# Order of the steps of branch A's attention on every engine, and plain copies for the first gates of branch B

## The reference

```python
proj = h @ w_in
qa, ka, va, qb, kb, vb, ga, gb = split(proj)
# branch A, 8 heads: two softmaxes (m = 0, 1) of 64 wide queries and keys per head, values 128 wide
s = einsum('bqhmd,bkhmd->bhmqk', qa, ka) * scale + bias      # keys of later chunks of 64 masked
p = softmax(s); attn = p[:, :, 0] - lam * p[:, :, 1]
ya = rmsnorm(einsum('bhqk,bkhe->bqhe', attn, va)) * subln_g * 0.8
# branch B: 16 query heads on 2 key heads, a window of 2 chunks, a sink in the denominator
merged = sigmoid(ga) * (ya @ w_branch_a) + sigmoid(gb) * (yb @ w_branch_b)
h = layer_norm(ALPHA * h + merged @ w_out)
h = layer_norm(ALPHA * h + square(relu(h @ w_ff1)) @ w_ff2)
```

## Time and profile before

| | |
|---|---|
| median of 3 runs | 1919.4 us (1918.81 to 1921.43) |
| the profiled execution | 1920.03 us, its span 1918.2 us |
| PE busy | 1827.2 us (95%) |
| DVE, ACT, POOL busy | 906.1, 609.1, 505.1 us |

### The profile page before, as it was taken

One profiled execution on the slowest core, in us unless ns is written; L12 is line 12 of the kernel. 1 busy time (PEld: TensorE's weight loads), 2 busy tenths in 40 slices (PEclk: granted clock), 3 DMA queues, 4 the chain that ended last, 5 costly groups with the idle time before them and its releaser, 6 DMA issues.

```text
span 1918.2 us, 24570 instructions
## 1 busy us (share of the span) xinstructions
PE 1827.2 (95%) x9174; PEld 1502.4 (78%) x9174; DVE 906.1 (47%) x2051; ACT 609.1 (32%) x1337; POOL 505.1 (26%) x306
## 2 busy tenths in 40 slices
PE   3999999999999997999999999999999999999995
PEld 2777777777778886888888788788888888888884
DVE  7276666666665553102422455433333333333337
ACT  4255555555556564311221211311111111111104
POOL 5111111111123442222221110633333333333324
PEclk9999999999999998999999999999999999999998
DMA  4511111111111100134322250311111111111102
GB/s 160 202 53 32 45 35 34 45 32 46 31 39 41 32 23 23 44 99 132 99 80 85 85 190 1 106 49 55 44 44 44 44 44 44 56 64 45 44 0 88
DMA packets 143108, 117.88 MB, mean 61 GB/s; under 512 B 23284, under 2 KB 129964, under 8 KB 143020
## 3 DMA queue, kind: packets, MB, share of 16 engines
q1 hardware_dynamic: 133804, 112.51, 18.5%
q10 hardware_dynamic: 9216, 4.20, 0.8%
HBM read 99.87 MB, written 21.53 MB: 63 GB/s over the span
## 4 chain that ended last, share of the span: by engine, by line
PE 80%; DVE 8%; ACT 5%; issue 2%; SPq 2%; POOL 2%; DMA 1%; POOLq 0%; DVEq 0%; ACTq 0%
PE bank L474 24%; PE bank L476 24%; PE bank L475 24%; PE bank L510 3%; PE bank L498 2%; PE bank L542 2%; ACT mix L832 1%; DVE mix L1185 1%; ACT mix L870 1%; DVE res L1121 1%; DVE mix L1236 1%; POOL w_lo L983 1%; PE bank L543 1%; SPq L336 1%; DVE o_buf L1163 1%
## 5 line engine op out<-in xcount | busy, mean ns | idle before, releaser
L474 PE MATMUL bank<-hT_hi,w_hi 128*128 128x512 f32 x1312 | 526.0, 401 | 13.8 <-POOL w_lo L983 6.4
L476 PE MATMUL bank<-hT_hi,w_lo 128*128 128x512 f32 x1312 | 513.9, 392 | 0.0
L475 PE MATMUL bank<-hT_lo,w_hi 128*128 128x512 f32 x1312 | 513.8, 392 | 0.0
L983 POOL TENSOR_TENSOR w_lo<-w_raw,w_hi 128x1024 fp32r<-128x1024 f32 x67 | 161.5, 2411 | 698.2 <-ACT w_hi L731 698.2
L474 PEld LDWEIGHTS bank<-hT_hi,w_hi 128*128 128x128 f32 x1312 | 248.1, 189 | 72.8 <-issue 9.5
L476 PEld LDWEIGHTS bank<-hT_hi,w_lo 128*128 128x128 f32 x1312 | 248.0, 189 | 53.6
L475 PEld LDWEIGHTS bank<-hT_lo,w_hi 128*128 128x128 f32 x1312 | 248.5, 189 | 48.3
L474 PE MATMUL bank<-y_hi 128*128 128x512 f32 (+1 forms) x604 | 228.0, 377 | 2.7 <-DVE small L1376 2.7
L475 PE MATMUL bank<-y_lo,y_hi 128*128 128x512 f32 (+1 forms) x604 | 225.1, 373 | 0.0
L476 PE MATMUL bank<-y_hi,y_lo 128*128 128x512 f32 (+1 forms) x604 | 225.0, 373 | 0.0
L1359 DVE TENSOR_TENSOR res<-res,bank 128x512 f32<-128x512 f32 x224 | 154.0, 687 | 141.3 <-PE bank L476 141.3
(11 more groups left out here) (133 smaller groups left out, 2636.6 us busy)
## 6 DMA issues: line engine op xcount, KB each, us to landing
w_raw<-in_w_in_dram SPq DMA_DIRECT2D x100, 256.0 KB, 3.3
w_raw<-in_w_ff_dram SPq DMA_DIRECT2D x64, 256.0 KB, 3.0
mix<-in_w_ff_dram SPq DMA_DIRECT2D x16, 1024.0 KB, 7.1
bias_rows<-bias_line SPq DMA_DIRECT2D x3, 1536.0 KB
res<-in_x_dram SPq DMA_DIRECT2D x8, 512.0 KB, 8.1
h_spill<-res SPq DMA_DIRECT2D x8, 512.0 KB, 6.8
o_spill<-o_buf ACTq DMA_DIRECT2D x64, 64.0 KB, 1.6
w_raw<-in_w_branch_b_dram SPq DMA_DIRECT2D x16, 256.0 KB, 3.9
```

Of the source, the lines that this page charges most:

```text
L474: pe.matmul(bank, lhs[0], rhs[0], start=start, stop=False)
L475: pe.matmul(bank, lhs[0], rhs[1], start=False, stop=False)
L476: return pe.matmul(bank, lhs[1], rhs[0], start=False, stop=stop)
L983: pool.tensor_tensor(w[1][:, n % 2], w_raw[:, :, :], w[0][:, n % 2].bitcast(F32), ALU.subtract).then_inc(w_lo_done, 1)
```

## The change

It has two parts.

In branch A a block's first half group now comes straight behind `block_a(0)`; then `block_a(1)` where there is one, then the transposes of the block before, then the product of the block *two* back, then a second half group where there is one. For this the transposed probabilities have a second buffer, `p_more`, in the memory of `res` rows 0 and 1, so ACT's wait for the spill of `res` now stands ahead of branch A, and `inv` has four slots instead of two. The `va` transposes move from the end of block 0 to block 1. On DVE the combination of a block moves behind the first reads of the next block's scores (`combine`). On ACT the exponentials go ahead of the copies for `i < 4`, behind them for `i >= 4`, and `out_rows` speaks of the block two back. The two products left over are made in branch B's steps 0 and 1.

In branch B the gate tiles 0 and 1 are copied out of PSUM without a sigmoid (`gate_raw`), the two halves of `gb 0` in steps 30 and 31; the sigmoid of both comes later, in place in `res`, behind the first `y_hi` copy that follows (`gates_set`). `yb_high(0)` and `yb_low(0)` are one step earlier, `yb_low(1)` stands ahead of the last low parts, the weights of `gb 2` are split right behind `yb_high(1)`, and the root moves behind the last `gb` tile.

```diff
@@ PE, branch A
                     block_a(0)
-                    prev = (h, i - 1) if i else (h - 1, NT - 1)
-                    if prev[0] >= 0:
-                        pe.wait_ge(probs_ready, prev[0] * NT + prev[1] + 1)
-                        for b in range(1 + prev[1] // 4):
-                            transposes(("pa",) + prev + (b,))
-                    if i >= 4:
-                        block_a(1)
-                    for _ in range(HALVES[i]):
+                    step = h * NT + i
+                    for piece in range(HALVES[i]):
                         group(*ORDER[6 * (h + 1) + at // 2], range(at % 2 * 4, at % 2 * 4 + 4))
                         at += 1
-                    if prev[0] >= 0:
-                        attend_a(*prev)
-                    if i == 0:
-                        pe.wait_ge(freed_act, freed(True, LAST[TILE[("va", h)]]))
-                        for b in range(2):
-                            transposes(("va", h, b))
+                        if piece == 0:
+                            if i >= 4:
+                                block_a(1)
+                            if step >= 1:
+                                pe.wait_ge(probs_ready, step)
+                                for b in range(1 + (step - 1) % NT // 4):
+                                    transposes(("pa", (step - 1) // NT, (step - 1) % NT, b))
+                            if step >= 2:
+                                attend_a((step - 2) // NT, (step - 2) % NT)
+                            if i == 1:
+                                pe.wait_ge(freed_act, freed(True, LAST[TILE[("va", h)]]))
+                                for b in range(2):
+                                    transposes(("va", h, b))
@@ DVE, branch A
+            def combine(n):
+
+                i, slot = n % NT, n % 2
+                dve.wait_ge(exp_done, n + 1)
+                if n >= 4:
+                    dve.wait_ge(sq_done, n - 3)
+                link(dve.reciprocal(inv[:, n % 4, :], sums[:, slot, :]))
+                link(dve.scalar_tensor_tensor(coef[:, slot:slot + 1], sums[:, slot, 0:1], neg_lam, inv[:, n % 4, 1:2], ALU.mult, ALU.mult))
+                p = [s_a[:, slot, m, 0:(i + 1) * P] for m in range(2)]
+                dve.scalar_tensor_tensor(p[0], p[1], coef[:, slot:slot + 1], p[0], ALU.mult, ALU.add).then_inc(probs_ready, 1)
+                dve.sem_inc(inv_ready, 1)
...
+                        if c == 0 and chunks == 2:
+                            combine(step - 1)
...
+                    if chunks == 1 and step >= 1:
+                        combine(step - 1)
@@ ACT, end of branch B
-                if s == B_STEPS - 1:
+                if s >= B_STEPS - 2:
                     act.wait_ge(yb_lo, 1)
-                    group_hi(TILE[("gb", 0)], 0)
+                    gate_raw(TILE[("gb", 0)], s - (B_STEPS - 2))
...
-                if s == B_STEPS - 3:
+                if s == B_STEPS - 4:
                     yb_high(0, B_STEPS - 5)
-            group_hi(TILE[("gb", 0)], 1)
             yb_high(1, B_STEPS - 1)
+            split_weights(TILE[("gb", 2)])
...
+            def gate_raw(n, half):
+                act.wait_ge(gemm_done, POS[(n, half)] + 1)
+                act.activation(res[:, TILES[n][1], half * HALF:(half + 1) * HALF], GEMM[POS[(n, half)] % 2][:, :], ACT.Copy).then_inc(freed_act, 1)
...
+                        if c == 2:
+                            act.wait_ge(freed_act, freed(True, POS[(TILE[("gb", 1)], 1)]))
+                            for n in range(2):
+                                act.activation(res[:, n, :], res[:, n, :], ACT.Sigmoid).then_inc(gates_set, 1)
@@ DVE, end of branch B
-                if s == B_STEPS - 2:
+                if s == B_STEPS - 3:
                     yb_low(0)
+            yb_low(1)
             probs_lo(B_STEPS - 1)
```

More of the change, by code:

```diff
@@ L312, in batch_views @@
                 c = min(4, i + 1 - 4 * b)
-                return [(pT[part][:, 4 * b:4 * b + c, :], bank[:, 0:c, :])]
+                return [(pT[i % 2][part][:, 4 * b:4 * b + c, :], bank[:, 0:c, :])]
             if kind == "pb":
@@ L818, in out_rows, with exp_a @@
                     store_rows(n - 1)
-            def prev_a(h, i, steps=NT):
-                return (h, i - 1) if i else (h - 1, steps - 1)
+            def exp_a(h, i):
+                act.wait_ge(max_ready, h * NT + i + 1)
+                for m in range(2):
+                    e = act.activation(s_a[:, i % 2, m, 0:(i + 1) * P], s_a[:, i % 2, m, 0:(i + 1) * P], ACT.Exp,
+                                       bias=neg_max[:, i % 2, m:m + 1], accum_out=sums[:, i % 2, m:m + 1])
+                e.then_inc(exp_done, 1)
+            act.wait_ge(spilled, 16 * NT)
             for h in range(A_HEADS):
@@ L825, in _ @@
                 for i in range(NT):
-                    prev = prev_a(h, i)
-                    if prev[0] >= 0:
-                        for b in range(1 + prev[1] // 4):
-                            batch_hi(("pa",) + prev + (b,))
-                    act.wait_ge(max_ready, h * NT + i + 1)
-                    for m in range(2):
-                        e = act.activation(s_a[:, i % 2, m, 0:(i + 1) * P], s_a[:, i % 2, m, 0:(i + 1) * P], ACT.Exp,
-                                           bias=neg_max[:, i % 2, m:m + 1], accum_out=sums[:, i % 2, m:m + 1])
-                    e.then_inc(exp_done, 1)
-                    for _ in range(HALVES[i]):
+                    step = h * NT + i
+                    if i < 4:
+                        exp_a(h, i)
+                    for piece in range(HALVES[i]):
                         if at % 2:
@@ L838, in _ @@
                         at += 1
[L839 to L843 removed]
+                        if piece == 0:
+                            if step >= 1:
+                                for b in range(1 + (step - 1) % NT // 4):
+                                    batch_hi(("pa", (step - 1) // NT, (step - 1) % NT, b))
+                            if i >= 4:
+                                exp_a(h, i)
+                            if step >= 2:
+                                out_rows(step - 2, (step - 2) // NT, (step - 2) % NT)
+                            if i == 1:
+                                for b in range(2):
+                                    batch_hi(("va", h, b))
                     splits_at = (1, 4, 5) if h == A_HEADS - 1 else (1, 4, 6)
@@ L927, in _ @@
                             group_hi(TILE[("g" + kind, c)], half)
+                if kind == "b":
+                    act.wait_ge(sq_done, A_HEADS * NT)
+                    act.activation(sq_sum[:, :, :], sq_sum[:, :, :], ACT.Sqrt, bias=eps, scale=1.0 / P).then_inc(y_norm, 1)
                 for c in range(KT):
@@ L1207, in _ @@
                         at += 1
-                    if prev[0] >= 0:
-                        sum_halves(step - 1)
-                    if i == 0:
-                        for b in range(2):
-                            batch_lo(("va", h, b))
+                        if piece:
+                            continue
+                        if step >= 1:
+                            for b in range(1 + (step - 1) % NT // 4):
+                                batch_lo(("pa", (step - 1) // NT, (step - 1) % NT, b))
+                        if step >= 2:
+                            sum_halves(step - 2)
+                        if i == 1:
+                            for b in range(2):
+                                batch_lo(("va", h, b))
             def probs_lo(s):
@@ L1289, in _ @@
                     gated("mb", c, half, mix)
+                if c == KT - 3:
+                    dve.wait_ge(y_norm, 1)
+                    link(dve.reciprocal(sq_sum[:, :, :], sq_sum[:, :, :]))
                 if c >= KT - 2:
```

60 lines of the change are left out of this document (22 added, 38 removed).

## The result

The changed kernel takes 1924.69 us (median of 17 runs, 1922.23 to 1927.27) against 1919.53 us for the kernel before (17 runs). The ratio is 1.0026, 95% interval 1.0019 to 1.0033. The forecast was 1915.1, in a range that holds 1924.69, but the sign is wrong: the kernel became slower by 5.2 us instead of faster by 4.3. The profiled execution has a span of 1922.9 us and a mean granted clock of 0.987. One execution of one experiment (the combination in its own block) took 2060.11 us at a mean granted clock of 0.849 and is left out of that experiment's time.

What follows compares the result with a forecast made beforehand. PE, busy 95% of the span, was taken as the bound, so only its waits and low clock could be won. Branch A +9.3 and end of branch B -13.6 gave -4.3 from 1919.4: 1915.1 us, range 1898 to 1926.

Steps and rivals of the forecast that it cites:

- Waits of branch A removed: Branch A: PE's waits for values' low parts, combination and score reads lose their cause where they stand, -22.5 us.
- Changes between kinds: Branch A: four more changes per head between kinds of matmul on PE, 0.15 us each, +4.8 us.
- My steps for a head: Branch A per head: waits removed, changes between matmul kinds, then new waits in blocks 2, 3 and 7.
- (a) Block 2: Branch A: PE waits 2.3 us in 7 heads, 1.5 in head 0, POOL's split holding DVE's `neg_max`; +17.6 us.
- (b) Block 3: Branch A: the delay goes on, `probs_ready` comes 0.45 us after PE wants it; +3.6 us over 8 heads.
- (c) Block 7: Branch A: POOL's split holds DVE at L1200, so PE waits 0.73 us, 8 times; +5.8 us.
- End of branch B: Stalls before `gb 1` and for `gb 2` weights go, the clock stays up, step 30's wait grows; -13.6 us.
- The wait before the transposes of step 30: End of branch B: `yb_low(0)` moved ahead of step 30's reads lengthens PE's 0.81 us wait to about 2.3; +1.5 us.
- the sum of branch A: Branch A: waits removed, changes between matmul kinds and new waits in blocks 2, 3 and 7 together, +9.3 us.
- R2: Branch A: lower clock follows the new waits, 1.8 to 3.0 us a fall, mostly 1924 to 1932 us; chance 0.17.

Runs made afterwards that it cites:

- the combination in its own block: Changed kernel with DVE's combination of every block moved back into that block, not behind the next block's reads: 1907.45 us (median of three).
- the run with two more reads: Changed kernel with block 1's weight split begun earlier, and DVE's read of block 2's second scores repeated twice more in each head: 1922.14 us.
- the run with the split early: Changed kernel with the weight split of block 1 begun earlier, ahead of `out_rows` and the values' high parts on ACT: 1905.98 us.
- The run with both splits early: Changed kernel with the weight splits of blocks 1 and 6 begun earlier, the latter ahead of block 6's exponentials: 1903.05 us.
- branch A alone: Changed kernel with the second part, the gates and the end of branch B, undone: 1938.27 us.

## Why the prediction was wrong

- **Waits of branch A removed, -22.5.** Right: none of the waits of the earlier trace rows is left where it stood. The 0.1 us beyond the idle time that each was to save was not measured.
- **Changes between kinds, +4.8.** Not measured alone. A head without falls costs, by the run with two more reads, 60.24 at an idle time of 1.79; with the changed kernel's 2.02 that is 60.47, which is 1.0 above before. My steps for a head (-2.8 + 0.6 + 2.3 + 0.45 + 0.73) gave 1.3. So without the clock the sum for a head was 0.3 too high.
- **(a) Block 2, 2.3 us.** Right: 2.40 from start to start, 2.2 in excess, with `neg_max` held for 1.60 us behind POOL. That the hold is the cause is shown by the run with the split early (0.17 us, 0.58 idle). The section "Who interferes with whom" of the page "SBUF — State Buffer" of the Trainium skill, which I had weighed in the prediction, says that a `tensor_scalar` can take the port pair that DVE shares with GpSimd, and that whichever comes second then stands until the first is done. The trace agrees, with the 1.60 us.
- **(b) Block 3, 0.45 us.** Wrong for the changed kernel, right in kind: the wait appears (0.29 idle) only where the clock doesn't fall. At half clock PE is slow enough for the combination to be ready.
- **(c) Block 7, 0.73 us.** Right in heads 0 to 6: 0.65 us in excess. The run with both splits early removes these seven waits and head 7's in block 6, 5.3 us of idle time.
- **End of branch B, -13.6.** Right: -13.9 by the starts, -13 alone. The wait before the transposes of step 30 is 2.29, forecast 2.3. But I gave that wait no price for the clock, and there I was lucky: of the eleven traces that have the wait, seven have a fall behind it, at 1.6 us, and the changed kernel's is one of the other four.
- **The step that failed** is the sum of branch A, which took the clock to stay up behind waits of 2.3 us. I had this as the rival R2, chance 0.17, and put it too low: the two falls I used followed 4.34 and 5.99 us, the one that stayed up 1.57, and I read the gap between them as if it favoured no fall. The kernel before had a third fall, behind 3.34 us at 1102.28, that I left out; it narrows the gap from above. The fall happens seven times, at 1.0 us each net of what block 3 then doesn't wait: +6.9 by the price in the run with two more reads, +6.7 by 61.43 against 60.47. My price of 1.8 to 3.0 a fall was too high, taken from falls that lasted 5.93 and 3.63 us of matmuls and hid no later wait, where those at step 30 cost 1.6 us; so R2 came true at 1924.7 and not at the 1939 that it gave for eight.
- **Not foreseen** is the entry of branch B. I walked the blocks of a head and never its last one, where no next block follows and branch B's scores come straight behind a half group. Wait and clock together are worth 3.5 us, by the run that reorders it.
- +6.9 and +3.5 equal the 10.4 us between +9.3 and +19.7. But the terms for a head were 0.3 too high, 2 us in all, so 2 us more are to be found. Head 7's wait in block 6, 1.45 us where I had counted 0.73, is 0.7 of them; 1.3 remain without a name. The 1.1 us won behind both branches is outside of every term. 10.4 less that, and less 0.3 at the end of branch B, are the 9.0 us between the span forecast, 1913.9, and the one measured, 1922.9.

## What to carry to other kernels

Price a new wait on PE in two parts: its length, and what PE's clock does behind it; here two microseconds once a head cost a microsecond more, while waits of 0.6 or 1.2 us in the same place cost nothing but themselves. Where one wait has been seen with and without a fall, put a chance on the second part, and before a difference of one or two microseconds is credited to an edit, see whether the two traces have their falls in the same places. When an engine's order is shifted, walk also the first and the last round of the loop, where the neighbour is another stage. Before moving a chain of small DVE operations, look at what POOL is doing over them: starting one POOL operation a few microseconds earlier turned this change from +0.3% to -0.7%.

## What the runs showed of the chip

- The granted clock fell to half, most often for about 3.4 us, behind 2.0 us of idle PE in seven of seven places of the changed kernel and in six of seven with branch A alone. Behind 1.65, 1.79, 2.2 to 2.3 and even 3.34 us it fell in some places and not in others with the same wait. Behind 1.57 us and less it never did between 83 and 1250 us. The net price was 1.0 us in a head and 1.6 us at step 30.
- The `TENSOR_SCALAR` on 128x2 numbers was held until POOL's operation was done (1.60 us against 0.17), behind a POOL memset as well (1.70 us), and so was a `SCALAR_TENSOR_TENSOR` on one number per partition (2.43 us against 0.22).
- Two effects were hidden in one place: the hold made the wait, and the wait made the fall. Taking the hold away gave back 2.40 us a head, of which the wait's own length is 1.4.
